# Distances between tiles and weights modulo 256 bytes in a kernel of two fused float32 blocks

## The reference

```python
q, k, v, g = jnp.split(h @ a_w_in[layer], 4, axis=-1)
o = chunked_relbias_attention(split_heads(q), split_heads(k), split_heads(v), a_rel_bias[layer]).reshape(b, s, D_INNER)
x = x + (o * jax.nn.silu(g)) @ a_w_out[layer]
...
k_s, v_s = jnp.split(h_kv @ kv_w, 2, axis=-1)
q, g = jnp.split(h @ b_w_in[lb], 2, axis=-1)
o = forgetting_attention(split_heads(q), k_sh, v_sh, cum_logf_h).reshape(b, s, D_INNER)
x = x + (o * jax.nn.silu(g)) @ b_w_out[lb]
```

## Time and profile before

| | us |
|---|---|
| median of 3 runs | 2482.94 (2482.22 to 2483.5) |
| the profiled execution | 2484.6 |
| its span, first to last instruction | 2483.0 |
| TensorE busy in the span | 2454.8 |
| VectorE, ScalarE, GpSimd busy | 1756.3, 1219.7, 303.6 |

### The profile page before, as it was taken

The page is one execution under the profiler, slowest core; times in us unless marked ns, Lnnn a source line. Parts: engine busy times, 40 slices in busy tenths (PEclk is TensorE's granted clock), DMA queues, the critical chain, the costliest instruction groups (busy, mean ns, idle before and its releaser), DMA issues.

```text
span 2483.0 us, 43962 instructions
## 1 busy us (share of the span) xinstructions
PE 2454.8 (99%) x16586; PEld 2188.3 (88%) x16586; DVE 1756.3 (71%) x2629; ACT 1219.7 (49%) x1811; POOL 303.6 (12%) x397
## 2 busy tenths in 40 slices
PE   8999999999999999999999999999999999999998
PEld 7999999888888888888888888888888888888887
DVE  8988797896767566656666668667576756676676
ACT  6555333665544445444444456545444444444445
POOL 1212114422100000000000001101010001000011
PEclk9999999999999999999999999999999999999999
DMA  7666763386566666666666665777667766766673
GB/s 217 173 160 169 195 182 87 104 220 192 171 185 195 187 180 175 189 174 191 177 187 191 176 173 165 191 190 181 192 175 190 195 181 184 189 182 179 191 194 103
DMA packets 758308, 442.79 MB, mean 178 GB/s; under 512 B 28784, under 2 KB 721136, under 8 KB 758160
## 3 DMA queue, kind: packets, MB, share of 16 engines
q1 hardware_dynamic: 752880, 430.16, 61.8%
q0 software_dynamic: 5280, 10.56, 3.2%
HBM read 437.35 MB, written 3.31 MB: 177 GB/s over the span
## 4 chain that ended last, share of the span: by engine, by line
PE 96%; DVE 2%; issue 1%; DMA 0%; ACT 0%; SPq 0%; DVEq 0%; ACTq 0%
PE bank L291 40%; PE bank L294 21%; PE bank L269 5%; PE bank L270 5%; PE bank L271 5%; PE bank L318 5%; PE bank L320 5%; PE bank L319 5%; PE bank L1851 1%; PE bank L1870 1%; PE bank L1858 1%; PE bank L1850 1%; PE bank L1871 1%; DMA rawa<-in_w_in_dram 0%; PE bank L1831 0%
## 5 line engine op out<-in xcount | busy, mean ns | idle before, releaser
L253 DVE TENSOR_TENSOR lob<-rawb,hib 128x1024 fp32r<-128x1024 f32 x672 | 834.8, 1256 | 374.9 <-ACT hib L246 369.0
L246 ACT ACTIVATE hib<-rawb 128x1024 fp32r<-128x1024 f32 x672 | 701.5, 1055 | 511.7 <-PE bank L294 349.3
L291 PE MATMUL bank<-xx,hib 128*128 128x512 f32 x3328 | 806.2, 392 | 0.0
L291 PEld LDWEIGHTS bank<-xx,hib 128*128 128x128 f32 x3328 | 608.9, 188 | 115.8 <-DVE mix L2140 0.2
L294 PE MATMUL bank<-xx,lob 128*128 128x256 f32 x3328 | 467.1, 287 | 0.7 <-DVE xx L2126 0.7
L294 PEld LDWEIGHTS bank<-xx,lob 128*128 128x128 f32 x3328 | 437.3, 191 | 19.4 <-DVE xx L2126 1.1
L269 PE MATMUL bank<-xh,hia 128*128 128x258 f32 (+2 forms) x1040 | 301.4, 290 | 10.5 <-DVE loa L253 10.2
L270 PE MATMUL bank<-xl,hia 128*128 128x258 f32 (+2 forms) x1040 | 296.3, 285 | 0.0
L271 PE MATMUL bank<-xh,loa 128*128 128x258 f32 (+2 forms) x1040 | 295.5, 284 | 0.0
L291 PE MATMUL bank<-oo,hib 128*128 128x512 f32 x1008 | 256.6, 393 | 0.0
L291 PEld LDWEIGHTS bank<-oo,hib 128*128 128x128 f32 x1008 | 181.8, 189 | 33.3
(11 more groups left out here) (294 smaller groups left out, 2264.5 us busy)
## 6 DMA issues: line engine op xcount, KB each, us to landing
rawb<-in_a_w_in_dram SPq DMA_DIRECT2D x256, 512.0 KB, 4.7
rawa<-in_w_in_dram SPq DMA_DIRECT2D x130, 512.0 KB, 5.3
rawb<-in_kv_w_dram SPq DMA_DIRECT2D x128, 512.0 KB, 4.4
rawb<-in_b_w_in_dram SPq DMA_DIRECT2D x128, 512.0 KB, 5.2
rawb<-in_a_w_out_dram SPq DMA_DIRECT2D x64, 512.0 KB, 5.0
rawb<-in_b_w_out_dram SPq DMA_DIRECT2D x64, 512.0 KB, 5.0
rawb<-in_w_out_dram SPq DMA_DIRECT2D x32, 512.0 KB, 4.9
table<-in_rel_dram POOLq DMA_DIRECT2D x32, 128.0 KB, 4.1
```

The lines of the kernel that those rows point to most:

```text
L246: nc.scalar.activation(self.hi[(2 * at.u + h) % SPL][:], self.raw_half(at, h), ACT.Copy).then_inc(hi_ready, 1)
L253: nc.vector.tensor_tensor(self.lo[b][:], self.raw_half(at, h), self.hi[b][:].bitcast(F32), ALU.subtract).then_inc(lo_ready, 1)
L291: last = nc.tensor.matmul(out, self.hi[b][:, w], both(k).rearrange("p a t -> p (a t)"), start=start and k == 0, stop=stop and not start an ...
```

## The change

It alters where tiles stand, and no instruction is added or taken away.

- The four `hi` and four `lo` buffers become longer by `room` elements, and buffer i begins `step * i` elements inside its own tile. Stream `b`: room 8, step 1, so 4128 bytes from tile to tile and 4 more inside, 36 bytes modulo 256 from buffer to buffer. Stream `a`: room 16, step 4, so 80 bytes modulo 256.
- The tiles of `xx0`, `xx1` and `oo` are 12 elements (48 bytes) longer: 2096 bytes from tile to tile. The hi and lo parts in a tile stay together.
- A spare tile of 1024 bytes ahead of `vv`, and `spare2` longer by 512 bytes, move the tiles of the first block behind them by multiples of 256.

```diff
-        def place_split(self):
-            self.hi = [sbuf(self.stack, f"hi{self.tag}{i}", [P, HALF], F32R) for i in range(SPL)]
-            self.lo = [sbuf(self.stack, f"lo{self.tag}{i}", [P, HALF], F32R) for i in range(SPL)]
+        def place_split(self, room, step):
+            def placed(name, i):
+                t = sbuf(self.stack, f"{name}{self.tag}{i}", [P, HALF + room], F32R)
+                return t[:, step * i:step * i + HALF]
+            self.hi = [placed("hi", i) for i in range(SPL)]
+            self.lo = [placed("lo", i) for i in range(SPL)]
...
     bk = sbuf(first, "bk", [P, CT, 2, LP])
+    spare = sbuf(first, "spare0", [P, 256])
     vv = sbuf(first, "vv", [P, CT, LP])
...
         st = Stream(ph, "a", 3, 0, sem("begin_in"))
-        st.place_split()
+        st.place_split(16, 4)
...
-    spare = sbuf(p2, "spare2", [P, 2792])
+    spare = sbuf(p2, "spare2", [P, 2792 + 128])
...
     st = Stream(ph, "b", 4, U_WOUT)
-    st.place_split()
-    xx1 = sbuf(ph, "xx1", [P, KT, 2, SEQ], F32R)
+    st.place_split(8, 1)
+
+    def spaced(name, tiles):
+        t = sbuf(ph, name, [P, tiles, 2 * SEQ + 12], F32R)
+        return t[:, :, 0:2 * SEQ].rearrange("p k (a t) -> p k a t", a=2)
+    xx1 = spaced("xx1", KT)
...
-    xx = [sbuf(ph, "xx0", [P, KT, 2, SEQ], F32R), xx1]
+    xx = [spaced("xx0", KT), xx1]
...
-    oo = sbuf(ph, "oo", [P, GH, 2, SEQ], F32R)
+    oo = spaced("oo", GH)
```

## The result

The changed kernel takes 2501.41 us (2500.08 to 2502.31), against 2482.94: the ratio is 1.0074, 95% interval 1.006 to 1.0088. It is slower by 18.5 us. The profiled execution took 2500.08 us, its span 2498.4; the profiled ones are 15.5 us apart (2484.6 before), and what is read from the traces stands against these.

What follows compares the result with a forecast made beforehand. TensorE's product spacing was taken to bound the kernel; gains of 9.0 + 4.6 + 1.8 + 4.3 = 19.7 us cut the 2483.0 us span to 2463.3, forecast as 2465 after giving a little back; range 2445 to 2500.

Steps and rivals of the forecast that it cites:

- pool of 116 us: TensorE's product spacings lie 11 to 14 ns above their floors, 116 us of the span, which the change reaches for.
- the address does count: First phase: products of the same form follow at 0.11 and 0.13 us, so addresses matter by some nanoseconds either way.
- Part 1: Wide products on xx, 3328 records: spacing from 228.1 to 225.4 ns, 9.0 us gained.
- Part 2: Wide products on oo, 1008 records: spacing from 230 to 225.4 ns, 4.6 us gained.
- Part 3: Turned units, 3 x 512 products: spacing from 226.6 to 225.4 ns, 1.8 us gained.
- Part 4: Narrow products, 3328 + 1008: spacing from 119.4 to 118.4 ns, 4.3 us gained.
- Part 5: First phase, weight buffers 80 bytes apart: between 1 ns better and worse, 3.1 us either way, taken as 0.
- Part 6: VectorE and ScalarE writing hi and lo at 4-byte starts: might slow, but VectorE's idle time covers it; cost 0.
- Part 7: Spare tiles and shifted allocations: no instructions and no transfer added or moved; cost 0.
- With no pattern to settle in: Wide products on xx: distance runs over sixteen values, so each takes its floor plus 9.6 ns, 225.4 ns.
- two passings: The stream passes the weights, modulo 256, about 2 times per load; the 11 ns surplus is the price.
- Rival A: Changing distances keep wide products unsettled at 232 ns, so the kernel is slower, 2502 us; chance 0.2.

Runs made afterwards that it cites:

- e3_first_only: Only the first phase's weight buffers stand 80 bytes apart modulo 256, the second block's spacing as in the kernel before; 2483.62 us, ratio 1.000 against that kernel.

## Why the prediction was wrong, point by point

- What bounds the kernel: right. TensorE waits for next to nobody in the second block before or after (nothing over 1.2 us), and the loss is spacing.
- The pool of 116 us and "the address does count": right that the address counts, by up to 7 ns a product.
- Part 1, 9.0 us gained on wide products of xx: this step failed, and the forecast with it. It had wide products at 225.4 ns, and they take 232.0; a run of 16 takes 3.71 us and not 3.61. The surplus of narrow products at changing distances (9.0 and 9.1 ns in the earlier trace rows) was carried over to wide ones (9.6). On the chip narrow products have their surplus nearly highest at 0 (9.9 ns, 5.9 at 192), wide and turned ones have it lowest at 0 (13.4 and 11.2; 17.0 at 192 for the wide). The two forms have their good values at different places, and at 0, where the kernel before stood, only the form that costs more stood well.
- Part 2, oo: 1.85 to 1.87 us for 8 and not 1.80. Part 3, turned: 232.8 and not 225.4, 9 us lost in place of 1.8 gained; the same step.
- Part 4, narrow: 119.1 to 118.6 on the mean, 16 of them 1.91 or 1.89 us as forecast; gained 2.7 us of 4.3.
- Part 5, first phase, 0: right (`e3_first_only`, ratio 1.000). Part 6, the starts of hi and lo: right, 1257 and 1057 ns. Part 7: right.
- "With no pattern to settle in": this is so (227.7 to 235.1 ns along the whole run), but the prediction took it as no loss. The fall inside a run had shown that the settled products are the cheap ones, at 226.6 to 227.7, and it was left out of part 1. At the other seven constants no place in the run behind the first product has a mean below 228.6.
- The estimate of two passings: one price for a passing can't be right, since at 192 narrow products have a surplus of 5.9 ns and wide ones of 17.0 with the same load beside them. What happens between the two streams stays open.
- The Trainium skill's rule, from "TensorE: Matmul & The Clock Gate", section "Part 2: What happens when you issue a matmul", that loading the next weights takes nothing from the running matmul: the runs speak against it. Moving xx and oo by 96 bytes, with every instruction the same, costs 1.3%, and wide and turned products, which have the two roles exchanged, take the same price at the same difference. No run leaves the loads out, so what the loading itself takes isn't shown.
- Rival A had 2502 us, its sign and its size (232 ns a wide product; measured 232.0). Its mechanism is what the changed kernel shows: its wide products stay as dear as the heads of the runs and never settle. What it lacked is that settling alone doesn't help: at 96, 192 and 224 they settle too, into patterns as dear. The range ended at 2500, below that rival's own number.

## What to carry to other kernels

When operands stand at one fixed distance modulo 256, spreading it gave here about the mean over the distances (wide products 231.5 to 232.0 ns, against a mean of 232.2 over eight constants). Find out by a few shifts of one tile whether the fixed distance is better or worse than that mean before anything is spread. Price each form of product by rows of its own form: here narrow and wide ones went opposite ways. And don't add up prices measured at constant distances: with lo alone at 192 two thirds of the turned products kept their distance and became 4 to 6 ns dearer.

## What the runs showed of the hardware that was not expected

- TensorE's products of 512 float32r columns follow at 227.0 to 234.2 ns (turned units at shifts 0 and 96) when nothing is moved but the tiles, at the upper clock level throughout (granted clock 0.998 and 0.999). A shift by 256 bytes moves nothing (`e3_first_only`).
- At one constant difference (192) narrow products stand at 115.1 ns and wide ones at 232.8, the lowest of eight for the one, near the highest for the other; at 64 both are low, and the turned ones pay.
- Products of one form whose addresses are equal modulo 256 can have more than one stable spacing (0.91 and 0.94 us for eight).
- Runs of 16 wide products settle into a flat spacing at difference 0 (226.7 ns from the sixth on) and into patterns of two or three products at others (231.8 and 234.9 in turn at 192).
- The whole kernel moves by 1.3% (2484.1 to 2517.7 us) when three tiles are shifted by 96 bytes, and by 0.7% (2501.3 us) with 32. An allocation that moves by 32 bytes as a side effect of another change can so hide or fake a gain.
